# Query transposes laid between gate products, one gate tile in two halves, bias products first in an expert block, one cache copy moved

## The chip, the cores and the metric

The kernel runs on one core of a Trainium2 chip. Its time is the device time of one execution in microseconds (us). The kernel before took 1348.09 us (median of 3 runs, 1347.71 to 1348.21). TensorE does the matrix products, VectorE and ScalarE empty the PSUM banks and do the elementwise work, GpSimd (POOL) does a few side jobs, and the sync engine (SP) issues nearly all DMAs, in order.

## What is computed

One inference step of a layer over 256 prompt tokens and 8 x 4 decode tokens, all in float32:

```
h = RMSNorm(x);  h @ w_in -> q, k, v of branches A and B, q of C, and 3 x 1024 gate logits
A: sliding window attention (128) with sinks     B: three dilated windows, combined
C: cross attention to 256 memory tokens
merged = sum over branches of sigmoid(gate_i) * (o_i @ w_br_i);   x = x + merged @ w_out
h2 = RMSNorm(x);  top-4 of 32 experts:
  gu = h2 @ w_gate_up[e] + b_gate_up[e];  act = (clip(up) + 1) * g * sigmoid(1.702 g)
  x = x + gate * (act @ w_down[e] + b_down[e]);    y = RMSNorm(x)
```

The caches of the decode tokens (2048 rows of branch B, 128 of A) are read for attention, and are also returned shifted by four rows, which is a plain copy in device memory.

## The kernel before

The five engines run streams written out by hand, tied by semaphores. TensorE's stream is this, in order:

1. Projections of the 288 tokens (lines 1013 and 1022), weights in blocks of 512 columns, two blocks resident at a time (`wblk`).
2. Gate logits: 24 tiles of 128 gate columns by 288 tokens, 8 products each (line 1038, `gate_tile`). Their weights are blocks 6 to 11, four tiles to a block. Each tile goes to PSUM bank 6 or 7 (`gate_bank`) and is emptied by ScalarE. Tiles serve as filler for TensorE's waits, so they lie in many places; the first `GATES_FIRST` = 4 come in one run here.
3. `TR_Q` = 13 groups of query and key transposes (line 980): three tiles of tokens with 15 transposes each in four groups, and one group of four for the memory keys. The groups alternate between banks 0 and 1, and a group waits until VectorE (line 1587) has emptied the group two before it. VectorE's rotary embedding (`rope_done`) must be finished for the tokens.
4. `NU` = 14 prompt attention units: A for units 0 to 3, B for 4 to 11, C for 12 and 13. In a unit u TensorE does one gate tile (not in the last), transposes the probabilities of u (line 1085), does the scores of u + 2 (line 1073; not in the last two), and the products with the values (line 1110, for C line 1102). ScalarE moves the transposed probabilities out (line 792) between lines 1085 and 1110. Units 12 and 13 have no scores there.
5. Decode attention: key transposes (line 1137) and scores (line 1153) per sequence, then values, with the other gate tiles among them.
6. Branch products, output projection (line 1279), router, ranks. A count product (line 1376) closes this.
7. 32 expert blocks of 64 rows. A block gathers its rows (`gather`, line 1389), transposes them (`x_transposes`, line 1400), does the 32 products of `gate_up` (line 1450; the trace has two records for each), four bfloat16 products that add the bias (line 1461), the transposes of the activations (line 1471) and 16 products of `down` (line 1489). Blocks are laid over one another: `down` of block b - 1 comes behind `gate_up` of block b. `scatter` (line 1434) adds finished pairs.

The expert weights, 12.6 MB a block, stream through seven slots of 2 MB. SP issues a load when TensorE has used the slot up (line 570): after two of the eight steps of `gate_up` (`gu_used`), or after a half of `down`.

SP's order around the change is: gate block 8 once gate tile 3 is done, a copy, then (once all transposes are emptied) the cache rows of sequences 0 and 1, the new keys and values out, two copies, gate block 9 once tile 7 is done, two copies, block 10, two copies, block 11, one copy, the two copies for branch A, and the cache rows of sequence 2 (line 497) once those of sequence 0 are used. Copies are line 475, gate weights line 457.

## Time and profile before

| | |
|---|---|
| median of 3 runs | 1348.09 us |
| the profiled execution | 1347.66 us, its span 1345.7 us |
| PE busy | 1297.3 us, 96% |
| DVE, ACT, POOL busy | 341.2, 213.0, 27.5 us |
| mean granted TensorE clock | 0.989 |
| DMA | 498.76 MB, mean 371 GB/s |

The span is what the trace covers; 1.96 us of the execution lie outside of it. A PE that is busy may still be slow, since the granted clock can be half. The chain of waits starts at the last instruction and goes back from each step to what released it, so its steps are the ones whose length sets the end.

### The profile page before, as it was taken

To read this page: it belongs to the slowest core of one execution; us is meant where nothing else is said; L and a number is where in the kernel's file an instruction comes from. 1 tells how busy PE (TensorE), PEld (TensorE's weight loads), DVE (VectorE), ACT (ScalarE), POOL (GpSimd) and SP (SyncE) were. 2 spreads that over 40 slices of the span, in tenths; PEclk is the share of its full clock that TensorE was granted. 3 is DMA by queue.
4 is the path that set the end of the run, shared out by engine and by line. 5 is a ranking of instruction groups with operands and counts; after the bars stand their busy time and mean duration, and the time that the engine had idled before them with its cause. 6 is when DMAs were issued, how large, how long until landed. Compare 5 with 4: busy or idle time off the path is not lost.

```text
span 1345.7 us, 14793 instructions
## 1 busy us (share of the span) xinstructions
PE 1297.3 (96%) x6332; PEld 540.7 (40%) x6332; DVE 341.2 (25%) x740; ACT 213.0 (16%) x442; POOL 27.5 (2%) x42
## 2 busy tenths in 40 slices
PE   7999998999999999999999999999999999999996
PEld 3446676667543333333333333333333333333332
DVE  2242443222543121212212122121212212121223
ACT  2211524323021111110111101111010111101012
POOL 0000002400000000000000000000000000000000
PEclk9999999999989999999999999999999999999998
DMA  6687877779939999999999999999999999999993
GB/s 249 248 304 303 275 292 246 234 234 319 386 130 360 398 429 428 428 427 428 427 427 428 428 428 428 428 428 428 427 428 428 428 427 427 428 427 427 428 427 159
DMA packets 71013, 498.76 MB, mean 371 GB/s; under 512 B 5808, under 2 KB 28976, under 8 KB 45584
## 3 DMA queue, kind: packets, MB, share of 16 engines
q1 hardware_dynamic: 70032, 495.15, 90.5%
q0 software_dynamic: 912, 2.62, 0.6%
q8 instruction: 52, 0.85, 0.3%
q14 instruction: 17, 0.14, 0.0%
HBM read 495.29 MB, written 36.96 MB: 396 GB/s over the span
## 4 chain that ended last, share of the span: by engine, by line
PE 80%; DMA 16%; DVE 2%; ACT 1%; issue 1%; SPq 0%; DVEq 0%
PE ps L1450 26%; PE ps L1489 13%; DMA ring<-in_w_gate_up 10%; PE ps L1038 7%; PE ps L1434 6%; PE ps L1389 5%; PE ps L1013 5%; DMA late<-in_w_gate_up 4%; PE ps L1279 2%; PE ps L1271 2%; PE ps L1153 2%; PE ps L1137 1%; PE ps L1400 1%; PE ps L1073 1%; PE ps L1471 1%; PE ps L1022 1%
## 5 line engine op out<-in xcount | busy, mean ns | idle before, releaser
L1450 PE MATMUL ps<-ring,cring 128*64 128x512 f32 x1760 | 400.7, 598 | 8.0 <-DMA ring<-in_w_gate_up 7.5
L1450 PEld LDWEIGHTS ps<-ring,cring 128*64 128x64 f32 x1760 | 120.4, 137 | 264.9 <-issue 240.7
L1489 PE MATMUL ps<-ring,cring 128*64 128x512 f32 x864 | 197.3, 598 | 2.0 <-ACT pT L915 1.3
L1841 DVE TENSOR_TENSOR cring<-ps,params 128x512 f32<-128x512 f32 x32 | 22.1, 692 | 438.5 <-PE ps L1400 438.5
L1939 DVE TENSOR_TENSOR x_tok<-x_tok,ps 128x1024 f32<-128x1024 f32 (+1 forms) x51 | 53.0, 1041 | 221.5 <-PE ps L1434 221.5
L1489 PEld LDWEIGHTS ps<-ring,cring 128*64 128x64 f32 x864 | 57.6, 136 | 118.0 <-issue 113.3
L1038 PE MATMUL ps<-hT,ring 128*128 128x288 f32 x384 | 100.2, 417 | 0.0
L906 ACT ACTIVATE cring<-ps 128x512 f32<-128x512 f32 x32 | 19.1, 597 | 496.2 <-PE ps L1471 496.2
L1389 PE MATMUL ps<-h_tok,cring 128*64 128x512 f32 x372 | 91.1, 607 | 0.0
L1038 PEld LDWEIGHTS ps<-hT,ring 128*128 128x128 f32 x384 | 72.9, 194 | 25.6 <-issue 6.6
L1013 PE MATMUL ps<-ring,hT 128*128 128x512 f32 (+3 forms) x240 | 73.0, 561 | 0.5 <-DVE hT L1589 0.5
L1450 PE MATMUL ps<-late,cring 128*64 128x512 f32 x288 | 69.5, 615 | 3.0 <-DMA late<-in_w_gate_up 2.0
L915 ACT ACTIVATE cring<-ps 64x512 f32<-64x512 f32 x32 | 18.9, 589 | 227.3 <-PE ps L1489 227.3
L1434 PE MATMUL ps<-cring 128*128 128x512 f32 (+1 forms) x96 | 52.6, 630 | 0.7 <-issue 0.7
L1434 PE MATMUL ps<-pT,cring 128*128 128x512 f32 (+1 forms) x96 | 49.3, 596 | 0.0
L1013 PEld LDWEIGHTS ps<-ring,hT 128*128 128x128 f32 (+1 forms) x240 | 32.7, 166 | 39.7 <-issue 38.8
L1854 DVE TENSOR_TENSOR cring<-cring 128x512 f32<-128x512 f32 x32 | 22.2, 693 | 85.6 <-ACT cring L902 85.6
L1389 PEld LDWEIGHTS ps<-h_tok,cring 128*64 128x64 f32 x372 | 21.1, 134 | 46.6 <-issue 42.8
L1450 PEld LDWEIGHTS ps<-late,cring 128*64 128x64 f32 x288 | 20.3, 141 | 47.1 <-issue 42.6
L1489 PE MATMUL ps<-late,cring 128*64 128x512 f32 x160 | 36.5, 598 | 0.0
L1279 PE MATMUL ps<-ring,hT 128*128 128x512 f32 (+1 forms) x96 | 33.4, 599 | 0.0
L898 ACT ACTIVATE cring<-ps 128x512 f32<-128x512 f32 x32 | 19.1, 597 | 90.0 <-PE ps L1389 85.7
(316 smaller groups left out, 951.0 us busy)
## 6 DMA issues: line engine op xcount, KB each, us to landing
ring<-in_w_gate_up SPq DMA_DIRECT2D x110, 2048.0 KB, 24.8
ring<-in_w_down SPq DMA_DIRECT2D x53, 2048.0 KB, 25.5
late<-in_w_gate_up SPq DMA_DIRECT2D x18, 2048.0 KB, 25.1
ring<-in_w_in SPq DMA_DIRECT2D x10, 2048.0 KB, 7.8
late<-in_w_down SPq DMA_DIRECT2D x10, 2048.0 KB, 25.5
out_dil_k_s<-in_cache_dil_k SPq DMA_DIRECT2D x8, 2044.0 KB
out_dil_v_s<-in_cache_dil_v SPq DMA_DIRECT2D x8, 2044.0 KB
cring<-in_cache_dil_k SPq DMA_DIRECT2D x8, 512.0 KB, 4.1
```

What stands on the lines that cost most here:

```text
L1013: ins = pe.matmul(bank((n % 2) * 3 + t)[k_rows(t, k), 0:b - a], hT_v[:, k, TOK0[t]:TOK0[t] + NTOK[t]], wblk[n % 2][:, k, 0:b - a], **k_gro ...
L1038: ins = pe.matmul(bank(gate_bank(m))[:, 0:TT], wblk[blk % 2][:, k, (m % 4) * P:(m % 4 + 1) * P], hT_v[:, k, :], start=(k == 0), stop=(k == ...
L1153: return pe.matmul(out, lhs, rhs, start=start, stop=last, skip_group_check=True)
L1271: ins = pe.matmul(bank(3 * (dt % 2) + br)[:, 0:TT], wblk[blk % 2][:, k, (dt % 4) * P:(dt % 4 + 1) * P], oT[:, k, :], start=(k == ks[0]), s ...
L1279: ins = pe.matmul(bank(wout_bank[t][n])[k_rows(t, k), :], hT_v[:, k, TOK0[t]:TOK0[t] + NTOK[t]], wo[n][:, k, :], **k_group(t, k))
L1389: ins = pe.matmul(bank(6)[64 * h:64 * h + 64, :], sel[0:n, t, :], h_v[0:n, t, h * 512:(h + 1) * 512], start=(t == 0), stop=(t == 2), skip_ ...
L1434: ins = pe.matmul(out, gateT[:, tok] if first else selT[:, tok], b_dn[:, 512 * h:512 * h + 512] if first else y2[h], start=True, stop=True ...
L1450: ins = pe.matmul(bank(gu0 + u)[64 * h:64 * h + 64, :], xTe[:, k % 4, (k // 4) * 64:(k // 4) * 64 + 64], pair_buf[slot][:, a:a + 512], sta ...
L1489: ins = pe.matmul(bank(5)[64 * h:64 * h + 64, :], aTe[:, kk % 4, (kk // 4) * 64:(kk // 4) * 64 + 64], pair_buf[slot][:, a:a + 512], start= ...
L1841: v.tensor_tensor(xTe4, xps, gain_x, ALU.mult).then_inc(S["xt_ready"], 1)
L1854: v.tensor_tensor(act, u_clip, g_sig, ALU.mult).then_inc(S["act_ready"], 1)
L1939: v.tensor_tensor(xs, xs, rows, ALU.add).then_inc(S["sc_added"], 1)
```

## The change

- The 13 groups of query transposes come first: two groups at once, then one group behind every second gate product. Three gate tiles are done in this stretch, where there were four ahead of the transposes.
- The units' gate tiles are thus numbered one lower (3 to 15). Tile 16 is done in units 12 and 13, half of its products in each, between the probability transposes and the values. Tile 3 goes to bank 7 where it went to 6.
- ScalarE evicts tile 16 in unit 13, ahead of that unit's output.
- The bias products are the first of a fixed expert block, ahead of its wait for `xt_ready`; in block 0 also ahead of `x_transposes(0)`. VectorE's activation waits for the last of the 32 products (`gu_used`). The dynamic overflow blocks, which don't run for these inputs, have them before the last step.
- The count product stands ahead of `gather_rows(1)`.
- One copy moves from behind gate block 11 to ahead of gate block 9.

```
-        GATES_FIRST = 4
+        GATES_FIRST = 3
-            return 6 if m in (1, 3, 18) else 7
+            return 6 if m in (1, 18) else 7
             copy_cache()
             copy_cache()
+            copy_cache()
             for i in (9, 10):
                 load_wblk(i)
                 copy_cache()
                 copy_cache()
             load_wblk(11)
-            copy_cache()
...
                 evict_pt(u)
+                if u + 1 == NU:
+                    evict_gate()
                 evict_o(u)
...
+            def gate_products(m, ks):
+                for k in ks:
+                    ins = pe.matmul(bank(gate_bank(m))[:, 0:TT], wblk[(6 + m // 4) % 2][:, k, (m % 4) * P:(m % 4 + 1) * P],
                                     hT_v[:, k, :], start=(k == 0), stop=(k == KC - 1))
-            for _ in range(GATES_FIRST):
-                gate_tile()
-            for n in range(TR_Q):
+            wblk_ready(pe, 6)
+            pe.wait_ge(S["proj_evicted"], 15)
+            q_transposes(0)
+            q_transposes(1)
+            for m in range(GATES_FIRST):
+                if m == 2:
+                    pe.wait_ge(S["gate_evicted"], 1)
+                for k in range(0, KC, 2):
+                    gate_products(m, (k, k + 1))
+                    n = 2 + 4 * m + k // 2
+                    if n < TR_Q:
+                        q_transposes(n)
...
                 p_transposes(u)
                 if u + 2 < NU:
                     scores(u + 2)
+                elif u + 2 == NU:
+                    split = gate_n[0]
+                    gate_n[0] += 1
+                    if split % 4 == 0:
+                        wblk_ready(pe, 6 + split // 4)
+                    pe.wait_ge(S["gate_evicted"], split)
+                    gate_products(split, range(KC // 2))
+                else:
+                    gate_products(split, range(KC // 2, KC))
                 values(u)
...
             def gate_up(b, gu0, one_hot):
+                fixed = isinstance(b, int)
+                if fixed and b >= 1:
+                    if b >= 2:
+                        pe.wait_ge(S["act_ready"], b - 1)
+                    gate_up_bias(gu0, one_hot, True)
                 pe.wait_ge(S["xt_ready"], b + 1)
...
-                for u in range(2):
-                    for h in range(2):
-                        ins = pe.matmul(bank(gu0 + u)[64 * h:64 * h + 64, :], one_hot,
-                                        bias_gu[0:96, u * D + h * 512:u * D + (h + 1) * 512], start=False, stop=True,
-                                        skip_group_check=True)
-                ins.then_inc(S["gu_done"], 1)
...
-            x_transposes(0)
             pe.wait_ge(S["bias_split"], 20)
             pe.wait_ge(S["ehot_ready"], 1)
+            gate_up_bias(0, expert_hot(0), True)
+            x_transposes(0)
             gate_up(0, 0, expert_hot(0))
...
-                v.wait_ge(S["gu_done"], b + 1)
+                v.wait_ge(S["gu_used"], 8 * b + 8)
```

How TensorE's rows move at three places. In the first, from the end of the projections on, L1022 is the memory projection, L1038 a gate product, L980 a transpose and L1073 the first scores. Before:

```order
L1022 MATMUL ps<-ring 128x512 x16
L1038 MATMUL ps<-hT,ring 128x288 x32
L980 MATMUL ps<-cst,cring 128x128 x12
L980 MATMUL ps<-cst,late 128x128 x3
L980 MATMUL ps<-cst,cring 128x128 x12
L980 MATMUL ps<-cst,late 128x128 x3
L980 MATMUL ps<-cst,cring 128x32 x12
L980 MATMUL ps<-cst,late 128x32 x3
L980 MATMUL ps<-cst,mkv_tok 128x128 x4
L1073 MATMUL ps<-late,qT 128x128 x8
```

All 49 transposes follow all 32 products. In the changed kernel the same things are L1024, L1043 and L982; the first eleven rows are:

```order
L1024 MATMUL ps<-ring 128x512 x16
L982 MATMUL ps<-cst,cring 128x128 x8
L1043 MATMUL ps<-hT,ring 128x288 x2
L982 MATMUL ps<-cst,cring 128x128 x4
L1043 MATMUL ps<-hT,ring 128x288 x2
L982 MATMUL ps<-cst,late 128x128 x3
L1043 MATMUL ps<-hT,ring 128x288 x2
L982 MATMUL ps<-cst,cring 128x128 x4
L1043 MATMUL ps<-hT,ring 128x288 x2
L982 MATMUL ps<-cst,cring 128x128 x4
L1043 MATMUL ps<-hT,ring 128x288 x2
```

It goes on in this way to the 24th product; two products stand between the last transposes and the scores. The second place is TensorE in units 12 and 13, from the last whole gate tile to the first key transposes of the decode stage. Before (L1085 probability transposes, L1102 values, L1137 key transposes):

```order
L1038 MATMUL ps<-hT,ring 128x288 x8
L1085 MATMUL ps<-cst,late 128x128 x8
L1102 MATMUL ps<-pT,mkv_tok 64x128 x8
L1085 MATMUL ps<-cst,late 128x128 x8
L1102 MATMUL ps<-pT,mkv_tok 64x128 x8
L1137 MATMUL ps<-cst,cring 128x128 x38
```

After, with L1043, L1102, L1119 and L1163 in their places:

```order
L1043 MATMUL ps<-hT,ring 128x288 x8
L1102 MATMUL ps<-cst,late 128x128 x8
L1043 MATMUL ps<-hT,ring 128x288 x4
L1119 MATMUL ps<-pT,mkv_tok 64x128 x8
L1102 MATMUL ps<-cst,late 128x128 x8
L1043 MATMUL ps<-hT,ring 128x288 x4
L1119 MATMUL ps<-pT,mkv_tok 64x128 x8
L1163 MATMUL ps<-cst,cring 128x128 x38
```

Four gate products stand in each of the two places where TensorE went from transposes straight to values. The third place is TensorE at the first expert block, from the last rank product (L1370) to the gather for block 1 (L1389). Before:

```order
L1370 MATMUL ps<-qT,cst 128x32
L1322 MATMUL ps<-h_tok,cring 64x512 x2
L1376 MATMUL ps<-cst,qT 32x1 x3
L1400 MATMUL ps<-cst,cring 128x128 x4
L1450 MATMUL ps<-late,cring 64x512 x8
L1450 MATMUL ps<-ring,cring 64x512 x24
L1461 MATMUL ps<-mkv_tok,late 64x512 x4
L1389 MATMUL ps<-h_tok,cring 64x512 x6
```

After (L1396 the rank product, L1399 the count, L1348 the gather of block 0, L1468 the bias, L1426 the row transposes, L1491 the products, L1415 the gather):

```order
L1396 MATMUL ps<-qT,cst 128x32
L1399 MATMUL ps<-cst,qT 32x1 x3
L1348 MATMUL ps<-h_tok,cring 64x512 x2
L1468 MATMUL ps<-mkv_tok,late 64x512 x4
L1426 MATMUL ps<-cst,cring 128x128 x4
L1491 MATMUL ps<-late,cring 64x512 x8
L1491 MATMUL ps<-ring,cring 64x512 x24
L1415 MATMUL ps<-h_tok,cring 64x512 x6
```

The count moved ahead of the gather, and the four bias products from behind the block's products to ahead of the row transposes.

## Rows read from the trace of the kernel before

**Rows 1.** Windows: us, busy time (instructions) per engine, PEclk granted, DMA share, GB/s.
```profile
396.00:402.60 6.60, 5.34 (x17) 2.16 (x17) 3.95 (x21) 1.92 (x3) 0.00 (x0) 0.50 0.00 0
...
460.00:900.00 440.00, 440.00 (x1966) 146.23 (x1964) 87.00 (x159) 47.74 (x84) 0.00 (x0) 1.00 1.01 428
```

**Rows 2.** Chain that ended last, 104 to 232 us: start, duration, what.
```profile
105.53 15.52 PE ps L1038 x64
...
130.11 2.77 PE ps L1073 x16
132.88 6.30 PE ps L1038 x16
...
142.53 4.08 PE ps L1038 x16
...
213.49 4.08 PE ps L1038 x16
...
219.55 1.58 PE ps L1102 x16
221.13 1.04 PE ps L1085 x8
...
223.27 1.59 PE ps L1102 x16
225.71 2.45 PE ps L1137 x19
```

**Rows 3.** Timeline at 120 us, the query transposes: start, duration, engine, line, [idle before].
```profile
120.88 1.04 PE L980 MATMUL ps<-cst,cring 128*128 128x128 f32 x8
...
121.59 1.29 DVE L1587 COPY qT<-ps 128x512 f32<-128x512 f32 x2 [21.77 <-PE ps L980]
```

**Rows 4.** Windows around the query transposes, and the decode key stage (242 to 270).
```profile
120.88:130.10 9.22, 6.54 (x50) 4.73 (x48) 6.71 (x13) 1.69 (x2) 0.00 (x0) 1.00 0.90 341
131.30:137.30 6.00, 6.00 (x21) 4.49 (x20) 4.78 (x13) 3.30 (x14) 0.00 (x0) 0.50 0.71 214
242.00:270.00 28.00, 27.33 (x395) 18.26 (x383) 7.90 (x12) 10.44 (x25) 9.07 (x12) 1.00 0.80 241
```

**Rows 5.** Timeline of VectorE and ScalarE in the first attention unit.
```profile
131.89 0.69 DVE L1657 TENSOR_TENSOR late<-ps,cst 128x512 f32<-128x512 f32 x1 [1.84 <-PE ps L1073]
...
133.94 0.40 ACT L774 ACTIVATE late<-late,stat 128x128 f32<-128x128 f32 x1 [11.15 <-DVE stat L1662]
...
136.40 0.69 DVE L1684 TENSOR_TENSOR late<-late,stat 128x512 f32<-128x512 f32 x1
...
139.21 0.41 ACT L761 ACTIVATE ring<-ps 128x288 f32<-128x288 f32 x1 [0.31 <-PE ps L1038]
...
139.65 0.60 ACT L792 ACTIVATE pT<-ps 128x512 f32<-128x512 f32 x1
```

**Rows 6.** Timeline of the load queue: the load of gate block 8.
```profile
121.08 0.37 SPq L457 DMA_DIRECT2D ring<-in_w_in  x1
```

**Rows 7.** Windows of 4 us: DMA while the attention units run.
```profile
156.00:160.00 4.00, 3.96 (x13) 2.15 (x14) 2.50 (x5) 1.19 (x3) 0.00 (x0) 1.00 0.00 0
```

**Rows 8.** Chain at the first expert block.
```profile
398.53 16.44 PE ps L1450 x64
414.96 0.43 PE ps L1461 x4
```

**Rows 9.** Timeline of TensorE ahead of the first expert block.
```profile
395.65 0.48 PE L1376 MATMUL ps<-cst,qT 128*32 128x1 f32 x6
396.41 1.13 PE L1400 MATMUL ps<-cst,cring 128*128 128x128 f32 x4 [0.28 <-ACT cring L898]
```

**Rows 10.** Chain in the last two expert blocks.
```profile
1276.39 3.65 PE ps L1450 x16
...
1294.13 3.78 PE ps L1450 x16
...
1299.83 3.58 PE ps L1450 x16
```

More of the change, by code:

```diff
@@ L1053, in _ @@
                 transposes(g)
+            wblk_ready(pe, 6)
[10 more added lines that the diff above has]
+                        q_transposes(n)
+            gate_n[0] = GATES_FIRST
             def scores(u):
@@ L1378, in _ @@
             ins.then_inc(S["cnt_done"], 1)
+            pe.wait_ge(S["hn_done"], 6)
+            pe.wait_ge(S["sel_ready"], 1)
+            gather_rows(1).then_inc(S["gath_done"], 1)
             def gather(b):
@@ L1437, in scatter, with gate_up_bias @@
                 ins.then_inc(S["sc_done"], 1)
-            def gate_up(b, gu0, one_hot):
+            def gate_up_bias(gu0, one_hot, start):
+                for u in range(2):
+                    for h in range(2):
+                        ins = pe.matmul(bank(gu0 + u)[64 * h:64 * h + 64, :], one_hot,
+                                        bias_gu[0:96, u * D + h * 512:u * D + (h + 1) * 512], start=start, stop=False,
+                                        skip_group_check=True)
+                return ins
+            def gate_up(b, gu0, one_hot):
+                fixed = isinstance(b, int)
[3 more added lines that the diff above has]
+                    gate_up_bias(gu0, one_hot, True)
                 pe.wait_ge(S["xt_ready"], b + 1)
-                if not isinstance(b, int) or b >= 2:
+                if not fixed:
                     pe.wait_ge(S["act_ready"], b - 1)
                 for k in range(KC):
+                    if k == KC - 1 and not fixed:
+                        gate_up_bias(gu0, one_hot, False)
                     slot, landed = pair_at("g", b, k // 2)
@@ L1451, in gate_up @@
                                             xTe[:, k % 4, (k // 4) * 64:(k // 4) * 64 + 64], pair_buf[slot][:, a:a + 512],
-                                            start=(k == 0), stop=False, skip_group_check=True)
+                                            start=(k == 0 and not fixed), stop=(k == KC - 1),
+                                            skip_group_check=True)
                     ins.then_inc(S["gu_used"], 1)
```

10 lines of the change are left out of this document (4 added, 6 removed).

## The prediction

> **What bounds the kernel now.** Three views, in this order. First the windows of the expert part [rows 1]: from 460 to 900 us the DMA share is 1.01 at 428 GB/s, so that the weight stream runs as fast as it ever does and TensorE's own pace there can't shorten anything. But from 396 to 402.6 us the DMA share is 0.00: all seven slots are full, and the next load waits until TensorE uses the first slot. The stream's end is therefore a fixed distance behind the moment at which the first expert block starts, and everything that reaches this moment sooner moves the end with it. Second, the chain from 104 to 232 us [rows 2]: it runs through TensorE, in gate products, transposes and attention, with waits between them. Third, the chain at the last two blocks [rows 10]: after the last real wait for a weight load, at 1276.39, it is TensorE's again, up to the small normalization at the end.
>
> So I count what the path of TensorE gains up to the first expert block, what the first blocks gain before the stream is full, and what TensorE gains behind the last load.
>
> **Query transposes between gate products.** Before: 32 gate products take 15.52 us from 105.53 on [rows 2], which is 0.485 each. The transposes begin at 120.88 [rows 3] and the first scores start at 130.11 [rows 2]. Eight full transposes take 1.04 us, 0.13 each [rows 3]; all 49 at that price (the 15 narrow ones can only be cheaper) are 6.4 us, so that of some 9.2 us about 3 are waits for VectorE's copies. In the window of the transposes PE is busy for 6.54 of 9.22 us [rows 4], which says the same. VectorE had been idle for 21.77 us when the first transposes ended [rows 3], so the rotary embedding was done by 99.8 and nothing keeps the transposes from starting at 105.5. A copy of a group takes 0.65 us (1.29 for two [rows 3]); now a group and two products, 0.5 + 0.97 us, pass before a bank is asked for again, so these waits go. The last copy has two products to hide behind.
>
> New length of this stretch: 24 x 0.485 = 11.6, plus 6.4, plus the 24 changes between products and transposes. The trace bounds a change at 0 (32 products and then transposes come without a gap at 120.88) and at 0.2 us (in the units a tile of eight products takes 4.08 with its change [rows 2], and 8 x 0.485 is 3.88); I take 0.05, nearer to the first, since most groups wait for nothing, which is 1.2 (0 to 4.8 for both ends). Sum 19.2, the scores start at 124.7: **5.4 us earlier**, with one gate tile less done. By the ends of the change's price: 6.6 to 1.8.
>
> **The clock and the first unit.** After the stretch with the waits the granted clock is 0.50 from 131.3 to 137.3, TensorE at 1.2 GHz, and at 1.00 before [rows 4]. There the gate tile of unit 0 takes 6.30 us where later ones take 4.08 [rows 2]. In the changed kernel TensorE has products all the way; the nearest row is the decode key stage, which alternates 19 transposes with scores, transposes being near half of its time, and was granted 1.00 through 28 us [rows 4]. So I expect no fall there.
>
> By the Trainium skill (TensorE: Matmul & The Clock Gate, the section Part 4: PE-mode transpose) a transpose does not count as TensorE being busy in the way a product does. The fall after a stretch of transposes alone agrees with that; it would also speak against diluting gate products with transposes. By it the sum would be that of the last rival below, by the key stage's row it is the forecast.
>
> What the full clock brings in unit 0 is less than its 3 us, because ScalarE is late next. From VectorE's first step, 131.89, to ScalarE's first exponential, 133.94, it is 2.05; ScalarE then works without a break until it evicts the gate tile at 139.21 and the transposed probabilities, 139.65 to 140.25 [rows 5]. That chain is 8.4 us from 131.89, and doesn't depend on TensorE's clock except through the gate tile, which is then ready before ScalarE wants it, so some 0.3 shorter: 8.1. One unit's scores at full clock are about 0.9 (2.77 for two units, most of it at half [rows 2]). So the values of unit 0 begin at 0.9 + 8.1 = 9.0 behind the start of the scores, and the next gate tile at 10.1 with 1 us of values; before it was 142.53 - 130.11 = 12.4 [rows 2]. **2.3 us earlier.** If the clock falls anyway: 0.
>
> **The gate tile in two halves.** It adds 8 x 0.485 = 3.9 us at the end of the prompt units. Before, TensorE stood still from 222.17 (221.13 + 1.04) to 223.27 waiting for ScalarE's copy, 1.1 us, and about the same ahead of 219.55, since the tile at 213.49 and eight transposes end at 213.49 + 4.08 + 1.04 = 218.6 [rows 2]. Each half, 1.94 + 0.1 for a change, covers 1.1 and adds 0.9: **1.9 us later** in all. ScalarE's eviction of the tile (0.41) lies beside the last values (1.59), so the output is not held up. With no cover at all it would be 4.1. The units before have the same tiles with other numbers; PE is busy throughout, and I count nothing.
>
> **Queues.** Gate block 8 is loaded once tile 3 is done: at 121.08 before [rows 6], now behind unit 0's tile, at about 130.5. SP is in order, so the copy, the cache rows of sequences 0 and 1 and the stores wait behind it; these cache rows are not used before 225.71, and tile 8 not before four more tiles of 4.08 us each. The moved copy makes three in a row behind the stores; at 156 to 160 the DMAs moved nothing [rows 7], so there is room, and the next gate block isn't asked for until tile 7 is done. It also leaves the queue emptier where the decode caches are loaded. I count 0 for all this; if the key stage does profit, it is by under 1 us.
>
> **Expert blocks.** Four bias products take 0.43 us [rows 8]. In block 0 they move behind the gather, where TensorE did the count product (0.48) and idled 0.28 for ScalarE [rows 9]; the count moves into the wait ahead of the gather. So block 0 is 0.4 shorter. In block 1 they come ahead of a like wait for VectorE's copy of the rows, so between 0 and 0.4 is won. In the full stream, blocks 2 to 29, the order inside a block costs or gives nothing. At the end the hard points are the waits for weights in block 30 (1276.39) and, 0.2 late (3.78 for 3.58), in block 31 at 1294.13 [rows 10]; the bias of block 31 used to come behind that and now is done before it: 0.4. Together **0.9 us earlier** (0.4 to 1.2).
>
> **The sum.** 5.4 + 2.3 - 1.9 + 0.9 = 6.7 us. The profiled execution took 1347.66 us (span 1345.7 and 1.96 around it); it lies 0.43 below the median of the runs, 1348.09. 1348.1 - 6.7 = 1341.4 us.
>
> **Rivals.**
> 1. The clock falls anyway near the first unit, because scores and small waits suffice. For it: the transposes remain a third of the stretch. Against it: the key stage. Then unit 0 gains nothing: 5.4 - 1.9 + 0.9 = 4.4, 1343.7 us.
> 2. More is gained: with the idle times at 218 to 226 filled, or merely since everything lies elsewhere in time, one of the other half-clock stretches is shorter. One is the 6.6 us at the entry of the first expert block at 0.50 [rows 1], where each us is worth half a us. Two to four us of such time less: 1339.5 us.
> 3. The end is pinned by the stream, whose loads before 396 would be late rather than waiting. Only the bias at the end is left: 1347.7 us, no measurable change. Against it stands the DMA share of 0.00 [rows 1].
> 4. Slower: the mixed stretch itself falls to 1.2 GHz, soon after 109 us, and stays there. It holds some 15.7 us of work at full clock, which would take 31.4; with unit 0 gaining nothing, the sum is -4.4 + 15.7 = 11.3 later, 1359.4 us. It decides from the point where 4.4 us of that work, 8.8 us of time, runs at 0.50. The key stage at 1.00 [rows 4] speaks against it.
>
> **Chances.** Forecast 0.50, rival 1 0.24, rival 2 0.12, rival 3 0.09, rival 4 0.05. A measurement of this kernel can tell 0.2%, 2.7 us, from no change. The first three cases lie beyond that on the fast side: 0.86 faster, 0.09 the same, 0.05 slower. The range for 8 in 10 covers the forecast with its unknown price per change (from +1.2 to -3.6), and rivals 1 and 2: 1338.0 to 1345.0.
>
> **What would show it.** First scores at about 124.7 us; windows of the mixed stretch at 1.00 and none at 0.50 around 131; the next gate tile some 10 us after the first scores; two gaps before line 1119 gone and the key transposes starting near 219.9, 5.8 earlier than 225.71; the first expert block 6 us earlier after a gather that bias products follow; 428 GB/s as before. Wrong would be: a half clock between 109 and 125, PE idle for VectorE's copies between groups, the scores starting later than 127, or a first expert block that starts earlier while the last weights land at the old time.

## The result and the profile after

The changed kernel takes 1338.05 us, the median of 6 runs (1334.93 to 1339.53). The kernel before, run on the same chip beside it, took 1347.9, the median of six runs, of which one of 1377.16 is in a slower state of the chip and is left out of the ratio (the median of the other five is 1347.71). The ratio is 0.9926, with a 95% interval of 0.9913 to 0.9938: **10.0 us faster** (8.4 to 11.7). The forecast was 1341.4, so the gain is half as large again as the 6.7 us of the sum, at the lower edge of the range.

The profiled execution took 1338.35 us, its span is 1336.5; before it was 1347.66 and 1345.7. The spans differ by 9.2 us. Two of the page's strips first, the whole span in 40 slices: the granted clock in tenths, and what the DMAs moved.

```profile
PEclk9999999999979999999999999999999999999999
GB/s 250 251 274 226 367 364 252 229 267 345 287 166 398 404 428 427 428 428 428 426 428 429 427 429 428 425 430 427 428 428 428 427 428 428 428 427 428 428 425 160
```

From the 15th slice on the stream runs at 428 GB/s, as before [rows 1]. The one dip of the clock, the twelfth slice, is the entry of the first expert block.

**The chain through TensorE**, start, duration and what, in the order of [rows 2]:

```profile
133.84 4.08 PE ps L1043 x16
...
209.75 1.94 PE ps L1043 x8
214.23 1.94 PE ps L1043 x8
218.54 2.45 PE ps L1163 x19
224.02 3.23 DMA cring<-in_cache_mem_k
227.28 2.45 PE ps L1163 x19
...
390.82 15.91 PE ps L1491 x64
```

L1043 is the gate product. The tile of unit 1 stands at 133.84 where it stood at 142.53, the two halves of tile 16 at 209.75 and 214.23, 1.94 us each, and the first key transposes at 218.54, 7.2 us ahead of 225.71 [rows 2]. The first expert block starts 7.7 us ahead of 398.53 [rows 8].

**The stretch of transposes and products.** A timeline: start, duration, engine, line, operation, and in brackets the idle time before and who ended it.

```profile
106.10 1.04 PE L982 MATMUL ps<-cst,cring 128*128 128x128 f32 x8
106.81 1.29 DVE L1624 COPY qT<-ps 128x512 f32<-128x512 f32 x2 [6.29 <-PE ps L982]
106.98 1.14 PE L1043 MATMUL ps<-hT,ring 128*128 128x288 f32 x4
107.95 0.60 PE L982 MATMUL ps<-cst,cring 128*128 128x128 f32 x4
108.39 1.14 PE L1043 MATMUL ps<-hT,ring 128*128 128x288 f32 x4
...
116.28 0.43 PE L982 MATMUL ps<-cst,cring 32*128 32x32 f32 x4
116.64 1.24 PE L1043 MATMUL ps<-hT,ring 128*128 128x288 f32 x4
117.81 0.43 PE L982 MATMUL ps<-cst,cring 32*128 32x32 f32 x4
...
123.75 1.71 PE L1090 MATMUL ps<-late,qT 64*128 64x128 f32 x16
125.38 4.15 PE L1043 MATMUL ps<-hT,ring 128*128 128x288 f32 x16
130.18 0.66 PE L1102 MATMUL ps<-cst,late 128*128 128x128 f32 x4 [0.65 <-DVE late L1721]
```

No row of TensorE has idle time before it until the first unit. A row's length runs to the end of its last instruction, which overlaps the next row, so a price is read from start to start. Two products take 0.97 us, from 106.98 to 107.95, and four transposes 0.44, from 107.95 to 108.39. The third tile's 15 transposes are narrow (32x32): four of them take 0.36, from 116.28 to 116.64, and two products between such groups 1.17, from 116.64 to 117.81. The scores start at 123.75, 17.65 after 106.10. The unit's tile begins at 125.38 and runs at full speed; it took 6.30 us before [rows 2]. At 130.18 TensorE already waits for VectorE's last step of the softmax, which follows ScalarE's exponentials; the prediction had a chain through both as the next thing late, and named ScalarE for it.

**The granted clock**, by windows: length, busy us (instructions) of PE, weight loads, DVE, ACT and POOL, then granted clock, DMA share and GB/s. The first two lie in the mixed stretch, among full and among narrow transposes, the third in the first unit, the fourth is the decode key stage, the last two the entry of the first expert block.

```profile
108.00:112.00 4.00, 4.00 (x24) 3.29 (x23) 2.04 (x4) 0.00 (x0) 0.00 (x0) 1.00 1.02 383
...
116.00:120.00 4.00, 4.00 (x23) 2.61 (x22) 0.78 (x3) 0.41 (x1) 0.00 (x0) 1.00 0.05 20
...
128.00:132.00 4.00, 3.35 (x17) 2.38 (x16) 1.92 (x7) 3.94 (x19) 0.00 (x0) 1.00 0.33 70
...
218.50:263.80 45.30, 43.52 (x641) 29.67 (x641) 13.30 (x20) 14.90 (x34) 21.89 (x31) 1.00 0.78 239
...
381.10:390.80 9.70, 8.71 (x29) 2.93 (x28) 2.21 (x10) 2.59 (x3) 0.35 (x1) 0.50 0.35 147
390.80:406.60 15.80, 15.78 (x66) 5.07 (x68) 3.22 (x20) 0.28 (x1) 0.00 (x0) 0.87 0.59 230
```

The half clock around 131 [rows 4] is gone. So is a second one that the prediction did not price, in the key stage. The kernel before, the whole key stage and the piece of it that holds the fall:

```profile
225.70:273.40 47.70, 44.94 (x641) 30.92 (x641) 13.30 (x20) 14.89 (x34) 21.87 (x31) 0.96 0.79 238
...
235.60:242.50 6.90, 6.89 (x76) 4.97 (x77) 2.08 (x3) 1.09 (x2) 6.32 (x11) 0.75 0.70 221
```

TensorE's wait for a key load ahead of that piece, and the same wait in the changed kernel:

```profile
235.61 3.69 PE L1137 MATMUL ps<-cst,cring 128*128 128x128 f32 x19 [2.04 <-DMA cring<-in_cache_mem_k]
```

```profile
227.28 2.44 PE L1163 MATMUL ps<-cst,cring 128*128 128x128 f32 x19 [0.89 <-DMA cring<-in_cache_mem_k]
```

At the entry of the first expert block the clock is still halved, and for longer: all of 9.7 us and, at a mean of 0.87, some 4 of the next 15.8, 13.7 us in all. It now begins at the gather, 9.7 us before the block's first product. Before, it began 2.6 us behind the gather's start and lasted some 10 us, the 6.6 of [rows 1] among them.

**Where the 9.2 us went.** The table cuts the span at the same events of TensorE in each kernel, all start times from its timeline. Each row is the time from the event of the row before to the one it names. E1 to E9 and C1 are the experiments below.

| until | before | after | C1 (after again) | E1 | E4 | E9 |
|---|---|---|---|---|---|---|
| end of projections (absolute) | 105.36 | 106.10 | 106.33 | 105.53 | 106.94 | 105.55 |
| first scores | 24.75 | 17.65 | 17.63 | 21.51 | 27.84 | 17.63 |
| gate tile of unit 1 | 12.35 | 10.02 | 10.05 | 10.03 | 10.03 | 10.06 |
| values of unit 12 | 77.09 | 77.85 | 77.85 | 77.08 | 77.08 | 77.84 |
| key transposes | 6.16 | 6.92 | 6.92 | 6.16 | 6.16 | 6.92 |
| gate tiles of the decode rows | 47.65 | 45.22 | 46.68 | 45.09 | 45.35 | 46.08 |
| gather of block 0 (two rows, the output projection between) | 117.3 | 117.3 | 117.3 | 117.3 | 117.3 | 117.3 |
| products of block 0 | 7.84 | 9.73 | 6.35 | 9.32 | 8.95 | 6.41 |
| gather for block 1 | 16.69 | 15.74 | 13.79 | 16.63 | 17.04 | 14.22 |
| first scatter | 12.96 | 12.94 | 12.94 | 12.95 | 12.94 | 12.95 |
| TensorE's end | 907.64 | 907.15 | 907.86 | 908.22 | 908.07 | 908.28 |

From before to after: +0.7 (the start varies by up to 3 us between kernels that are equal up to there), −7.1, −2.3, +0.8, +0.8, −2.4, 0, +1.9, −1.0, 0, −0.5.

### The profile page after: what moved, and what is told of

It reads as the page before. It is cut to its first block, busy times and chain, and to the rows that moved or that the text cites. A ratio compares the mean times of both kernels' runs of the same rounds, so it can differ in the third digit from the quotient of the medians.

```text
span 1336.5 us, 14794 instructions
## 1 busy us (share of the span) xinstructions
PE 1294.5 (97%) x6332; PEld 535.9 (40%) x6332; DVE 341.4 (26%) x740; ACT 212.9 (16%) x442; POOL 27.5 (2%) x42
## 4 chain that ended last, share of the span: by engine, by line
PE 80%; DMA 16%; DVE 2%; ACT 1%; issue 1%; SPq 0%; DVEq 0%
PE ps L1491 26%; PE ps L1525 13%; DMA ring<-in_w_gate_up 10%; PE ps L1043 7%; PE ps L1460 6%; PE ps L1415 5%; PE ps L1015 5%; DMA late<-in_w_gate_up 4%; PE ps L1305 2%; PE ps L1297 2%; PE ps L1426 1%; PE ps L1507 1%; PE ps L1179 1%; PE ps L1090 1%; PE ps L1163 1%; PE ps L1024 1%
## 5 line engine op out<-in xcount | busy, mean ns | idle before, releaser
L1491 PE MATMUL ps<-ring,cring 128*64 128x512 f32 x1760 | 400.5, 598 | 8.0 <-DMA ring<-in_w_gate_up 8.0
L1491 PEld LDWEIGHTS ps<-ring,cring 128*64 128x64 f32 x1760 | 119.9, 137 | 255.1 <-issue 226.5
L1043 PE MATMUL ps<-hT,ring 128*128 128x288 f32 x384 | 100.6, 412 | 0.0
L1415 PE MATMUL ps<-h_tok,cring 128*64 128x512 f32 x372 | 91.1, 607 | 0.0
L1043 PEld LDWEIGHTS ps<-hT,ring 128*128 128x128 f32 x384 | 70.4, 190 | 23.0 <-issue 5.9
L1491 PE MATMUL ps<-late,cring 128*64 128x512 f32 x288 | 69.0, 611 | 2.8 <-DMA late<-in_w_gate_up 2.0
L1415 PEld LDWEIGHTS ps<-h_tok,cring 128*64 128x64 f32 x372 | 21.1, 134 | 47.1 <-issue 43.4
L1491 PEld LDWEIGHTS ps<-late,cring 128*64 128x64 f32 x288 | 19.9, 140 | 45.1 <-issue 38.4
```

The source lines that it names most:

```text
L1043: ins = pe.matmul(bank(gate_bank(m))[:, 0:TT], wblk[(6 + m // 4) % 2][:, k, (m % 4) * P:(m % 4 + 1) * P], hT_v[:, k, :], start=(k == 0), s ...
L1415: ins = pe.matmul(bank(6)[64 * h:64 * h + 64, :], sel[0:n, t, :], h_v[0:n, t, h * 512:(h + 1) * 512], start=(t == 0), stop=(t == 2), skip_ ...
L1491: ins = pe.matmul(bank(gu0 + u)[64 * h:64 * h + 64, :], xTe[:, k % 4, (k // 4) * 64:(k // 4) * 64 + 64], pair_buf[slot][:, a:a + 512], sta ...
```

## The experiments

Two theories were set against each other from the start. By the theory, order alone does it: products fill the waits for VectorE's copies, and with the waits goes the half clock. The rivals: the clock follows from where the transposes lie in time and not from the waits; the split tile, the bias products or the moved copy bring the gain; and the surplus over 6.7 is a chance of the clock. Ratios are to the kernel before on the same chip, medians with a 95% interval.

**E1: the order of the transposes alone.** Kernel before, with the transposes between the gate products, four tiles first as before, no split tile, no other edit.

```
-            for _ in range(GATES_FIRST):
-                gate_tile()
-            for n in range(TR_Q):
+            q_transposes(0)
+            q_transposes(1)
+            for m in range(GATES_FIRST):
+                if m >= 2:
+                    pe.wait_ge(S["gate_evicted"], m - 1)
+                for k in range(0, KC, 2):
+                    gate_products(m, (k, k + 1))
+                    n = 2 + 4 * m + k // 2
+                    if n < TR_Q:
+                        q_transposes(n)
```

> The kernel before with one part of the change: the transposes are laid between the products of the first gate tiles, but four tiles stay in this stretch, as before, and no tile is split. Theory (the waits for VectorE's copies and the half clock behind them were what the reordering removed): from the end of the memory projection to the first scores 24 x 0.485 for three tiles, 5.8 for the transposes and 3.9 for the fourth tile, 21.4 us where it was 24.6; unit 0 2.3 shorter; together 5.5 us less than before. If the shorter key stage (2.4 us) of the changed kernel comes from this reordering too, 7.9 less. Rival (the gain lies in the split tile that fills the waits of the last units): under 4 us less, and the half clock still there behind the transposes.

Measured: 1342.84 us over 8 runs, ratio 0.9967 (0.9950 to 0.9983). By the table the stretch is 3.2 us shorter, unit 0 another 2.3, and the key stage 2.6; at the expert entry the half clock is now the long one, +1.4. The three gains are as large as in the changed kernel once the tile that E1 does first, 3.9 us, is counted: 21.51 − 3.88 = 17.63. So the order of the transposes brings the first two, and in this profile the key stage is short as well. The span is 6.0 us shorter; the median says 4.4 (2.3 to 6.7), less than the 5.5 to 7.9 expected.

**E2: the bias products alone.** Kernel before, with the expert part of the change.

```
-            x_transposes(0)
             pe.wait_ge(S["bias_split"], 20)
             pe.wait_ge(S["ehot_ready"], 1)
+            gate_up_bias(0, expert_hot(0), True)
+            x_transposes(0)
             gate_up(0, 0, expert_hot(0))
...
-                v.wait_ge(S["gu_done"], b + 1)
+                v.wait_ge(S["gu_used"], 8 * b + 8)
```

> The kernel before with only the expert part of the change (bias products first, count product earlier). Theory: block 0 0.4 us shorter and 0.4 to 0.5 at the end behind the last load, 0.9 us less in all, nothing else moved. Rival (the stream pins the end and only the part behind the last load counts): 0.4 less. Rival (the bias products hold the half clock or delay the first use of a slot): 0 to 1 more.

Measured: 1344.98 us over 12 runs, ratio 0.9979 (0.9965 to 0.9993), 2.8 us below the kernel before. Its profile doesn't show such a gain. Block 0 with the gather behind it takes 24.03 us against 24.53, and the rest to the end 908.58 against 907.64; the span is 1346.3, longer than before. The edit's own half a us is there, and 0.44 at the end (below, with E9); the median's 2.8 are not accounted for by them. The profiled run, 1348.16, is one of the two slowest of the 12. E9 asks again from the other side. In this profile the key stage takes 47.59 us and has the half clock of the kernel before in it.

**E3: the moved copy put back.** Changed kernel, with the cache copy behind gate block 11 again.

```
             copy_cache()
             copy_cache()
-            copy_cache()
             for i in (9, 10):
                 load_wblk(i)
                 copy_cache()
                 copy_cache()
             load_wblk(11)
+            copy_cache()
```

> The changed kernel with the one cache copy back in its old place behind gate block 11. Theory (the copy is beside the path in either place): within 0.3 us of the changed kernel, 9.5 us less than before, and the key stage as short as there. Rival (the copy out of the way is what shortened the key stage): 1 to 2.4 us slower than the changed kernel, with a later landing of the cache rows of sequence 2.

Measured: 1342.76 us over 9 runs, ratio 0.9961 (0.9944 to 0.9978). In the profile the key stage takes 52.26 us against 45.22 in the changed kernel, and nothing else behind the start moves by more than 0.4. By the medians the kernel is 4.7 us slower than the changed one; neither the 0.3 nor the 1 to 2.4 expected covers that. The chain of E3 has the load of the decode keys in it:

```profile
223.37 7.54 DMA cring<-in_cache_mem_k
```

The same piece was 3.23 in the changed kernel. That load is issued behind the copy on the same queue; what the copy costs there is taken up with the repetition below.

**E4: the waits filled, the order kept.** Kernel before, with one more gate product's worth of TensorE work ahead of each of 11 waits for a copy. The products write a bank whose content is not used.

```
+                    pe.matmul(bank(5)[:, 0:TT], ident, hT_v[:, 0, :], start=True, stop=True)
```

> The kernel before, its order untouched, with one more product (128 x 288, 0.485 us, into a bank that nobody reads) ahead of each of the 11 transpose groups that wait for a copy: work is added, and only the idle time goes. Theory (the half clock at 131 comes from the waits in the stretch of transposes): 5.3 us of products into some 3 us of waits, the first scores 2.3 to 3 us later, no half clock behind it and unit 0 2.3 us shorter: -0.3 to +0.8 us in all. Rival (the clock falls by its own, or because of the transposes themselves): half clock still there, +2.3 to +3 us.

Measured: 1348.79 us over 12 runs, ratio 1.0006 (0.9993 to 1.0018). Windows of E4, the transposes and the first unit:

```profile
122.60:134.80 12.20, 11.42 (x73) 8.17 (x70) 7.00 (x13) 1.69 (x2) 0.00 (x0) 1.00 0.89 343
134.80:144.80 10.00, 9.34 (x46) 6.49 (x46) 5.74 (x14) 5.67 (x24) 0.00 (x0) 1.00 0.76 243
```

The same 49 transposes stand behind the same products, in the same part of the span, and the clock is 1.00 where it was 0.50 [rows 4]. Unit 0 takes 10.03 us instead of 12.35. The 11 fillers cost 3.1 us and give back 2.3. In the three profiles whose waits are open (the kernel before, E2, E7) unit 0 takes 12.35 us, and in the eleven others 10.02 to 10.06. What fell before was therefore the clock behind a stretch of transposes with open waits, and products in the waits suffice against it. Whether the standing still or the lack of products lowers it isn't told apart, since the fillers are products. Filling them with work that has to be done anyway is the changed kernel.

**E5: without the split tile.** Changed kernel, with four tiles in the mixed stretch and units 12 and 13 as before.

```
-        GATES_FIRST = 3
+        GATES_FIRST = 4
...
-                elif u + 2 == NU:
-                    split = gate_n[0]
...
-                    gate_products(split, range(KC // 2))
-                else:
-                    gate_products(split, range(KC // 2, KC))
```

> The changed kernel without the split tile: four gate tiles between the transposes, none in units 12 and 13; copy moved, bias products first. Theory (each half covers a wait of 1.1 us, so that the tile costs 1.5 us there and 3.9 in the first stretch): 2.3 us slower than the changed kernel, first scores 3.9 later, the last two units 1.5 shorter, key stage as short as there (45.2 us). Rival (the halves, by filling the waits ahead of the key stage, are what keeps the clock up there): 4 to 5 us slower, key stage 47.6 us with a half clock in it.

Measured: 1340.54 us over 4 runs, ratio 0.9935 (0.9910 to 0.9960). The chain of E5 at the last two units (L1117 values) and the first load behind them:

```profile
215.67 1.58 PE ps L1117 x16
219.39 1.59 PE ps L1117 x16
...
227.30 3.10 DMA cring<-in_cache_mem_k
```

The values are 3.72 us apart where they are 4.48 apart with a half tile between (214.23 to 209.75 above, the halves being ahead of the values). So splitting costs 0.76 in each of two units, 1.52, and saves the 3.86 us of the tile ahead: 2.3 us net. Its span is also 2.3 longer than the changed kernel's, but by chance: it started 0.9 later, was 1.6 shorter at the expert entry, where its half clock lasted less, and 0.6 longer behind it. The medians differ by 2.5, within their intervals. Its key stage is as short as the changed kernel's, 45.29, without the halves ahead of it.

**E7: the copy moved alone.** Kernel before, with the third cache copy ahead of gate block 9 and none behind block 11.

```
+            copy_cache()
             for i in (9, 10):
...
             load_wblk(11)
-            copy_cache()
```

> The kernel before with nothing but the cache copy moved ahead of gate block 9. Theory (before, the copy starts 16.1 us ahead of the reload of the key cache and has passed; only the renumbered tiles bring it to 11.7 us and into its way): same as before within 0.5 us, key stage 47 to 48 us, reload landing in about 4 us. Rival (the copy hinders the key cache also before): 1 to 3 us faster than before, the last row of the reload landing 3.2 us behind its issue, no half clock in the key stage.

Measured: 1348.87 us over 10 runs, ratio 1.0001 (0.9989 to 1.0012). The key stage and its first load in E7:

```profile
228.30:274.00 45.70, 43.39 (x640) 29.59 (x640) 13.29 (x20) 14.90 (x34) 21.86 (x31) 1.00 0.78 237
```

```profile
233.74 3.95 DMA cring<-in_cache_mem_k
```

The load lands in the same time as before, 4.03 there. Alone, the move of the copy is worth nothing by the medians. But this execution had no half clock in the key stage, and the stage took 45.72 us where 47 to 48 were expected and the kernel before took 47.65. That is what the rival expected to see. Whether the copy's place or chance did it, one profile can't tell: E1 and E4 have the copy in its old place and no half clock in the stage either.

**E6 and E8: products in the waits at the expert entry.** The half clock there was the one part that got worse. E6 is the changed kernel with three products of constants into a bank that is free (288, 128 and 256 columns), behind the transposes, behind the last router step and behind the row transposes of block 0. E8 has 512, 512 and 256 columns and 512 more ahead of the gather.

```
+            def fill(n):
+                pe.matmul(bank(3)[:, 0:n], const("ones"), const("mask_b", P)[:, 0:n], start=True, stop=True)
...
+            fill(288)
...
+            fill(128)
...
+            fill(256)
```

> The changed kernel with three extra products (288, 128 and 256 columns wide, into a bank that nobody reads) in TensorE's waits ahead of the first expert block: ahead of the last router products, ahead of their sum, and behind the row transposes of block 0. Theory (the half clock of 13.7 us at the entry comes from the waits and narrow products there, and filling the waits is enough): no or a shorter half clock, from the gathers to block 0 7 us where it is 9.7, block 0 14 us where it is 15.7, 3 to 4.5 us faster than the changed kernel. Rival (narrow products are what lowers the clock, and the waits are too little to matter): half clock as before, 0 to 1 us slower.

> As the kernel with three extra products at the entry, but wider ones: 512, 512 and 256 columns, and one of 512 more ahead of the gathers of block 0, about 2.1 us of added work of which 1 lies in waits. Theory: the half clock is gone and, net of 1 us of work, 2 to 3.5 us faster than the changed kernel. Rival: half clock all the same, 1 to 3 us slower.

Measured: E6 1336.75 us over 4 runs, ratio 0.9912 (0.9890 to 0.9935), span 1333.9; E8 1336.30 over 4, ratio 0.9906 (0.9890 to 0.9923), span 1334.5. In both the clock stays at 1.00 at the entry: block 0 and its gather take 6.35 + 13.78 us instead of 9.73 + 15.74, 5.3 less. E8 pays 1.3 us of that back in front of the gather. By the medians they are 1.3 and 1.8 us below the changed kernel, less than expected, and neither is clearly below it, whose own interval reaches to 0.9913. So the changed kernel was run again beside a longer series of E6.

**C1, E9, E3 and E6 again, five rounds on one chip.** C1 is the changed kernel, unedited. E9 is the changed kernel with the bias and count products back in their places (the reverse of E2's diff). E3 and E6 are as above.

> The changed kernel again, beside the three that follow on the same chip. Theory: 0.992 to 0.994 of the kernel before, 8 to 10.5 us less; the half clock at 131 never there, the one at the entry of the expert blocks 10 to 14 us long. Rival (the first comparison caught lucky placements of the half clock): 5 to 7 us less.

> The changed kernel with the expert part undone: bias products last in a block, count product behind the gather. Theory: 0.4 us at block 0 and 0.4 to 0.5 at the end, 0.9 us slower than the changed kernel, blocks between unchanged. Rival (the bias products at the entry lengthen the half clock there): 0 to 2 us faster.

> The changed kernel with the copy back behind gate block 11, again, now beside the changed kernel. Theory (the copy starts 12 us ahead of the reload of the key cache where the kernel before had 16 us, and is in its way): 3 to 6 us slower than the changed kernel, key stage 48 to 52 us, reload landing 6 us or more behind its issue. Rival (that was one run's accident): within 1 us.

> The changed kernel with the three products in the waits ahead of the first expert block, again, now beside the changed kernel. Theory: no half clock at the entry, 2 to 4 us faster than the changed kernel. Rival (only in some runs): less than 1 us.

| kernel | median us (runs) | ratio, 95% | span | key stage | block 0 + gather |
|---|---|---|---|---|---|
| before | 1347.58 (17) | | | | |
| C1, changed | 1338.48 (6) | 0.993 (0.991 to 0.995) | 1333.6 | 46.68 | 20.14 |
| E9, bias back | 1335.45 (6) | 0.9929 (0.9908 to 0.9951) | 1333.2 | 46.08 | 20.63 |
| E3, copy back | 1344.77 (12) | 0.9975 (0.9959 to 0.9990) | 1346.0 | 52.28 | 25.26 |
| E6, products at the entry | 1334.88 (6) | 0.9915 (0.9897 to 0.9932) | 1332.2 | 46.44 | 20.14 |

*The copy.* E3 again: 6.3 us over C1 by the medians, and its interval lies wholly above C1's. The spans differ by more, 12.4, since E3's profile is its slowest run, with a later start and the long half clock at the entry. The timeline of its load queue around the end of the units, where L475 is the copy that was put back and L497 the first of the decode stage's key loads:

```profile
211.38 0.59 SPq L475 DMA_DIRECT2D out_dil_v_s<-in_cache_dil_v  x1
...
223.06 0.38 SPq L497 DMA_DIRECT2D cring<-in_cache_dil_k  x1
```

Its chain and one row of its timeline:

```profile
226.34 7.61 DMA cring<-in_cache_mem_k
233.99 4.32 PE ps L1163 x19
```

```profile
233.99 2.40 PE L1163 MATMUL ps<-cst,cring 128*128 128x128 f32 x10 [5.54 <-DMA cring<-in_cache_mem_k]
```

TensorE stands still for 5.54 us, and then works at half clock: 19 key transposes take 4.32 where they take 2.45. The load it waits for, 256 KB, is one of those that follow L497 on the queue. The copy, 2044 KB, was issued 11.7 us ahead of the first of them (211.38 to 223.06). In the kernel before the two are 16.1 us apart, and the same load lands in 4.03:

```profile
212.07 0.59 SPq L475 DMA_DIRECT2D out_dil_v_s<-in_cache_dil_v  x1
...
228.18 0.38 SPq L497 DMA_DIRECT2D cring<-in_cache_dil_k  x1
```

```profile
231.54 4.03 DMA cring<-in_cache_mem_k
```

In E1 they are also 16.1 apart, and its chain has

```profile
225.79 3.31 DMA cring<-in_cache_mem_k
```

So 11.7 us gave 7.54 and 7.61; 16.1 us gave 4.03, 4.32 (E2) and 3.31, and no copy behind block 11 gave 3.10 to 4.68 in the seven other profiles whose chain goes through this load. It isn't the only thing that can delay one: in E6's first profile the second load of its kind, issued at 228.62, took 6.51 with no copy there, and the stage 46.49. The reason for the shorter distance is the renumbering of the tiles. Gate block 11 can be loaded once tile 15 is done, and with three tiles first instead of four that is a unit later; the key rows are asked for at an hour that the same change has made earlier. In the changed kernel the queue's rows are

```profile
208.90 0.37 SPq L457 DMA_DIRECT2D ring<-in_w_in  x1
...
221.00 0.38 SPq L497 DMA_DIRECT2D cring<-in_cache_dil_k  x1
```

with the gate block at 208.90 and behind it only the two copies of 496 KB that every version has. Whether the load is late because the copy's packets are ahead of it in the queue or because the copy shares the memory was not told apart.

*The bias products.* E9 against C1, windows of the wait and of block 0. C1:

```profile
382.80:389.10 6.30, 4.95 (x29) 2.02 (x28) 2.18 (x10) 2.59 (x3) 0.35 (x1) 1.00 0.54 226
389.10:402.90 13.80, 13.76 (x64) 4.65 (x66) 3.23 (x20) 0.28 (x1) 0.00 (x0) 1.00 0.67 262
```

E9:

```profile
381.40:387.80 6.40, 4.51 (x25) 1.73 (x24) 2.20 (x10) 2.61 (x3) 0.37 (x1) 1.00 0.54 225
387.80:402.00 14.20, 14.18 (x68) 4.88 (x70) 3.21 (x20) 0.28 (x1) 0.00 (x0) 1.00 0.68 268
```

The four products, 0.43 us, move from the second window to the first, where TensorE is busy for only 4.5 of 6.4 us. That is 0.49 at the entry (20.63 − 20.14), and the tail from the first scatter to TensorE's end is 0.42 shorter in C1 than in E9, where the chain of E9 still has the bias product behind each block's last weights:

```profile
1263.86 3.65 PE ps L1476 x16
1267.51 0.43 PE ps L1487 x4
```

The tail as a whole differs by up to 2.6 us between profiles, though, so the end is better measured from the last wait for weights [rows 10], in the changed kernel's first profile and in E9:

```profile
1285.41 3.76 PE ps L1491 x16
```

```profile
1281.60 3.76 PE ps L1476 x16
```

TensorE ends at 1326.66 and 1323.28. From that wait to the end it is 41.23 to 41.26 us in all nine profiles with the bias products first and 41.68 to 41.70 in all five with them last: 0.44. Together 0.9 us, as priced. The medians can't show it: E9's is 3 us under C1's, while the means of their six runs are 1337.1 and 1337.3 us, and E2's lies 2.8 us the other way by its ratio. What E2's median shows beyond its segments stays open.

*The clock at the entry.* In C1 and E9 there is no half clock at the entry without any filler (the windows above, 1.00), against what was expected for C1 and although it is the changed kernel of the first profile, where it was 0.50 there. So the +0.9 us of the first profile is not a property of the change. E6 in this series:

```profile
381.60:387.90 6.30, 5.36 (x31) 2.21 (x30) 2.21 (x10) 2.56 (x3) 0.32 (x1) 1.00 0.56 229
387.90:401.70 13.80, 13.79 (x65) 4.65 (x66) 3.21 (x20) 0.28 (x1) 0.00 (x0) 1.00 0.67 264
```

The mean granted clock was 0.994 to 0.997 in each of E6's six runs and 0.991 to 0.998 in C1's, three of them at 0.991. E6 is 3.6 us below C1 by the medians and 2.0 by the means, and their intervals overlap. With E8 (0.9906) it is the fastest version run here, 11.4 to 12.7 us below the kernel before in its two series (0.9912 and 0.9915); that it beats the changed kernel is likely and not shown.

## What the prediction had right, and the steps that failed

The direction, the path and the mechanism of each priced term were right. Two steps failed: the price of the mixed stretch (5.4 us of gain, measured 7.1), and the count of 0 for the decode key stage (measured 1.0 to 2.4).

**What bounds it: right.** The first expert block starts 7.7 us earlier, and from the first scatter on the time is the same to 0.5 us (907.64 and 907.15). The stream ran at 428 GB/s as before [rows 1], so its end moved with the entry. Rival 3, the stream pinning the end, is out.

**The first step that failed: "all 49 at that price".** Priced at 5.4, measured 7.1; right in kind, 1.7 us too small. The 0.13 us of a transpose was read from the length of a row, 1.04 for eight [rows 3]. The changed kernel has the same row at 106.10, and its next product starts at 106.98: 0.88, so 0.11 each. The 34 full transposes thus take 3.7 us and the 15 narrow ones 1.4, together 5.1 where the prediction took 6.4. That is 1.3 of the difference. The 24 changes, 1.2 us in the prediction, took 0.9, and not evenly: among full transposes two products take 0.97, which is just twice 0.485, so that a change costs nothing, while two products between narrow transposes take 1.17, 0.1 more for each change, as does the change to the scores. The stretch of 17.65 us is so 11.64 of products, 5.1 of transposes and 0.9 of changes. The prediction's 19.2 stands 1.55 over it; the remaining 0.2 is where the old stretch was taken to begin (105.53 there, 105.36 here).

**Clock and unit 0: right.** 2.33 measured, 2.3 priced, and the segment is 10.02 to 10.06 us in all eleven profiles in which the transposes were mixed in or the waits filled. E4 shows the cause: with the waits filled and nothing moved, the clock stays at 1.00. So rival 1 and rival 4 are out, and with them the reading of the Trainium skill (TensorE: Matmul & The Clock Gate, Part 4: PE-mode transpose) that transposes not counting as busy would dilute the products: in the mixed stretch they are 5.1 of 17.65 us, and the clock is 1.00 in every window of it. The Trainium skill may still be right on transposes alone with gaps between them; E4 put products into those gaps and doesn't separate the two.

**Two halves of a tile: right.** Priced at 1.9, measured 1.52; each half costs 0.76 where 0.9 was expected. The two gaps ahead of the values are gone from the chain: TensorE goes from a half tile, 214.23 + 1.94, to the values and to the key transposes at 218.54. E5 shows what the sum left implicit: against doing the same tile ahead of the units, splitting saves 2.3 us.

**The second step that failed: "I count 0 for all this; if the key stage does profit, it is by under 1 us."** It profited by 2.4 in the profile, in two parts. TensorE waited 0.89 us for a key load where it had waited 2.04, 1.15 less (the chain's load landed in 3.23 rather than 4.03). The rest, some 1.3, is the half clock at 235.6 to 242.5 of the kernel before (0.75 over 6.9 us), gone after the change. In C1 the load took 4.68 and TensorE waited longer than before:

```profile
229.19 2.44 PE L1163 MATMUL ps<-cst,cring 128*128 128x128 f32 x19 [2.55 <-DMA cring<-in_cache_mem_k]
```

The stage took 46.68 there, still 1.0 less than before, since the clock stayed up. In the seven profiles of the changed kernel and of its variants with the copy moved (the first one, C1, E5, E6 twice, E8, E9) the stage took 45.2 to 46.7, 46.0 in the mean; with the old order and the copy in its old place it took 47.65 and 47.59 (E2), both with the half clock. So the term is about 1.6 us and not 0. The shorter wait varies from run to run. What keeps the clock up in the stage stays open: E7, the old order with the copy moved, had no half clock there either (45.72), nor had E1 and E4 with the copy in its old place. With three profiles of the old order, two of them with the half clock, chance isn't excluded.

The count of 0 for the copy was right only for the difference between the two kernels. It hid two things that cancel: without the copy's move the changed kernel is some 5 to 6 us slower (E3: 4.7 and 6.3 by the medians in two series), which goes with the renumbering of the tiles, and moving the copy gives them back. The prediction looked for room at 156 to 160 us, where the copy goes [rows 7], and not at the place it leaves. There the trace of before could have warned: the copy at 212.07 and the load at 228.18 were 16.1 us apart, and a tile numbered one lower brings the copy nearer to the load.

**Expert part: right by the segments, 0.9 us**, 0.49 at the entry and 0.44 at the end, and not visible in medians of six.

**The whole.** From the profiled spans: −9.2 measured against −6.7, made of −1.7 in the stretch, −0.4 in the halves, −2.4 in the key stage, +0.7 at the start and +1.3 in the expert part, where the half clock at the entry was longer. The parts that repeat, 1.7, 0.4 and about 1.6, are 3.7 us; the median's gain of 10.0 is 3.3 more than the sum's 6.7. Rival 2 put more half clock gone at 1339.5 with a chance of 0.12, and its mechanism had a hand in it at the key stage; at the entry, where it looked for it, the profile shows the opposite and the repetition shows none at all. (By its own price of half a us for each us of half clock, two to four us less would be 1340.4 to 1339.4, so its figure is the far end.)

## What to carry to other kernels

Work that must be done anyway, put into another operation's waits, pays twice here: the waits go (24.75 − 3.88 − 17.65 = 3.2 us of the stretch), and the clock that would have fallen behind the waits doesn't (2.3 us, shown alone by E4). When an order or a numbering changes, follow each large DMA that hangs on it to the small load behind it on the same queue, and compare the distance before and after; a moved DMA that is worth nothing in the old order (E7) was worth some 5 to 6 us in the new one (E3). Gains smaller than the spread that the clock makes, here 7 us between runs of the changed kernel and 10 between runs of the kernel before, are better read from segments of the trace between the same two events than from medians.

## What the runs showed of the hardware that was not expected

- **The clock differs between runs of one kernel.** The changed kernel's 12 runs lie between 1332.8 and 1339.9 us, and their mean granted clocks between 0.990 and 0.998. The clocks of its two profiles differ in one place, the entry of block 0 (0.50 in one, 1.00 in the other), worth 5.3 us. A line fitted through the time against the lost clock, (1 − clock) x span, over 17, 28 and 13 runs of the kernel before gives 0.66, 0.72 and 0.47 us for each us lost.
- **Products in the waits go with a full clock.** With 11 products of about 0.485 us in a stretch of 12.2 us (E4) the half clock behind the transposes was gone; it was there in all three profiles with open waits. With three products of 128 to 288 columns in the waits at the entry of block 0 (E6, and wider ones in E8) it was absent in all three profiles, but also in two of the eleven without them. No run of E6 or E8 had a mean clock of 0.992 or less, where half of C1's had.
- **TensorE changes between 128x128 transposes and 288-column products at no cost**: two products with their changes take 0.97 us, twice 0.485. Between 32x32 transposes they take 1.17.
- **A row of matmuls is longer than its turn.** Eight transposes make a row of 1.04 us, and the next product starts 0.88 behind their start.
- **A copy's harm depends on its distance.** Issued 11.7 us ahead of the key loads on the same queue, a copy of 2044 KB made one of 256 KB land in 7.54 and 7.61 us instead of 3.10 to 4.68; issued 16.1 us ahead it did not (4.03, 4.32 and 3.31).
